# Attention of a hybrid transformer block: values become the stationary operand in two parts, the turned exponentials stream past them

## The reference, cut to what matters

```python
def window_sink_attention(q, k, v, kc, vc, sink):      # "A": 3 local key tiles + 2 context tiles
    ...
    s_loc = jnp.where(mask[None, :, None, None], s_loc, -jnp.inf)
    p = jax.nn.softmax(jnp.concatenate([s_loc, s_ctx, s_sink], -1), -1).astype(v.dtype)
    out = (jnp.einsum('bnkgqs,bnskd->bnqkgd', p[..., :w], vw)
           + jnp.einsum('bnkgqc,bckd->bnqkgd', p[..., w:w + lc], vc))

def global_block_attention(q, k, v, kc, vc):           # "B": all 8 + 2 key tiles
    def one_block(qblk):
        s = jnp.einsum('bqkgd,bskd->bkgqs', qblk, k_all).astype(F32)
        p = jax.nn.softmax(s, -1).astype(v_all.dtype)
        return jnp.einsum('bkgqs,bskd->bqkgd', p, v_all)

def ctx_attention(q, k, v, sink):                      # "C": context queries on 2 context tiles
    s = jnp.einsum('bqkgd,bskd->bkgqs', (q * ATTN_SCALE).reshape(bsz, lc, nkv, grp, hd), k)
    p = jax.nn.softmax(s, -1)[..., :lc].astype(v.dtype)
    return jnp.einsum('bkgqs,bskd->bqkgd', p, v)
```

## Time and profile before

| | |
|---|---|
| time, median of 3 runs | 3813.87 us (3808.86 to 3818.49) |
| the profiled execution's own time | 3815.01 us |
| its span | 3813.2 us |
| busy in the span: PE / DVE / ACT / POOL | 88% / 49% / 22% / 36% |
| mean granted clock | 0.944 |
| attention of layer 0: first score matmul, last exponentials | 262.2 us, 525.4 us |
| attention of layer 1: first score matmul, last output | 2284.9 us, 2528.3 us |

### The profile page before, as it was taken

How to read it: one execution, slowest core, us unless ns; L and a number is a source line. 1 busy time by engine, 2 the same in 40 slices (tenths; PEclk the granted TensorE clock), 3 DMA queues, 4 the chain that set the end, 5 groups by cost and what they waited for, 6 DMA issues and landing times. The chain is left out here.

```text
span 3813.2 us, 47769 instructions
## 1 busy us (share of the span) xinstructions
PE 3362.3 (88%) x17208; PEld 2793.3 (73%) x17208; DVE 1866.7 (49%) x2854; ACT 846.7 (22%) x1574; POOL 1386.0 (36%) x1032
## 2 busy tenths in 40 slices
PE   0969989877979999999997669989787799999997
PEld 0849878655858888888884549878666578888885
DVE  8976534678582222222227886525675532222225
ACT  1136432212041010000003226432211220010102
POOL 1354222253324333343432254213242344444443
PEclk9979999988989999999998789999888899999998
DMA  7500002002301111111011410011002011111111
GB/s 278 171 17 1 0 30 65 6 20 89 118 28 39 39 39 39 33 41 42 33 33 67 171 61 1 0 39 56 6 14 86 33 40 49 50 50 50 44 50 50
DMA packets 63857, 197.74 MB, mean 52 GB/s; under 512 B 6160, under 2 KB 16656, under 8 KB 62736
## 3 DMA queue, kind: packets, MB, share of 16 engines
q1 hardware_dynamic: 54736, 172.32, 13.3%
q10 hardware_dynamic: 9024, 24.14, 1.8%
HBM read 177.05 MB, written 19.40 MB: 52 GB/s over the span
## 5 line engine op out<-in xcount | busy, mean ns | idle before, releaser
L188 PE MATMUL ps<-h_hi,f_whi 128*128 128x512 f32 (+1 forms) x1760 | 650.8, 370 | 26.5 <-DVE h_lo L1917 19.7
L189 PE MATMUL ps<-h_lo,f_whi 128*128 128x512 f32 (+1 forms) x1760 | 650.0, 369 | 0.0
L190 PE MATMUL ps<-h_hi,f_wlo 128*128 128x512 f32 (+1 forms) x1760 | 649.4, 369 | 0.0
L2145 DVE TENSOR_TENSOR f_gated<-f_gated,ps 128x512 f32<-128x512 f32 (+1 forms) x110 | 69.6, 634 | 973.8 <-PE ps L190 968.5
L2029 POOL TENSOR_TENSOR f_whi<-f_wraw,small 128x1024 fp32r<-128x1024 f32 x128 | 251.8, 1967 | 608.1 <-PE ps L190 608.1
L2153 DVE SCALAR_TENSOR_TENSOR x_res<-ps,mod,x_res 128x512 f32<-128x512 f32 (+1 forms) x440 | 306.8, 697 | 242.2 <-PE ps L190 241.9
L188 PEld LDWEIGHTS ps<-h_hi,f_whi 128*128 128x128 f32 x1760 | 333.3, 189 | 85.8 <-issue 22.2
L190 PEld LDWEIGHTS ps<-h_hi,f_wlo 128*128 128x128 f32 x1760 | 333.0, 189 | 55.8
L189 PEld LDWEIGHTS ps<-h_lo,f_whi 128*128 128x128 f32 x1760 | 333.3, 189 | 55.2
L188 PE MATMUL ps<-f_ahi,f_whi 128*128 128x512 f32 (+1 forms) x880 | 328.3, 373 | 0.0
L189 PE MATMUL ps<-f_alo,f_whi 128*128 128x512 f32 (+1 forms) x880 | 323.5, 368 | 0.0
(11 more groups left out here) (219 smaller groups left out, 6212.8 us busy)
## 6 DMA issues: line engine op xcount, KB each, us to landing
f_wraw<-in_w_ffn SPq DMA_DIRECT2D x132, 512.0 KB, 3.2
ada_w<-in_w_ada SPq DMA_DIRECT2D x80, 512.0 KB, 3.5
wrawc<-in_w_in SPq DMA_DIRECT2D x26, 512.0 KB, 3.8
wrawab<-in_w_in SPq DMA_DIRECT2D x16, 512.0 KB, 4.4
wrawo<-in_w_out SPq DMA_DIRECT2D x16, 512.0 KB, 3.4
ada_w<-in_w_ada ACTq DMA_DIRECT2D x16, 512.0 KB, 4.4
x_res<-in_xT SPq DMA_DIRECT2D x8, 640.0 KB, 6.5
x_spill<-x_res ACTq DMA_DIRECT2D x8, 640.0 KB, 5.6
```

Source lines behind the costliest of these rows:

```text
L188: pe.matmul(out, w_hi, h_hi, start=first, stop=False)
L189: pe.matmul(out, w_hi, h_lo, start=False, stop=False)
L190: return pe.matmul(out, w_lo, h_hi, start=False, stop=last)
L2145: dve.tensor_tensor(g, g, pl.bank(3 + c, tn), ALU.mult).then_inc(u_taken[c], 1)
```

## The change

The value matmul is turned round. The values are stored in two float32r parts side by side, the rounded value and the rest, 64 + 64 columns: `v_tok` is now `[P, group, tile, kv head, 128]`. They are the stationary operand. The turned exponentials too are split in two parts, `turned[:, t, 0, :]` (rounded) and `turned[:, t, 1, :]` (the rest), 256 columns that stream past. One float32r matmul per key tile gives the four products, with the value parts on the partitions and the exponentials' parts in the columns. ACT copies this 128 x 256 block out of bank 7 to `quarters`, and two float32 matmuls with the constant `joiner` (two identities over each other) add the four quarters and bring the queries back to the partitions, in bank 6.

In the unit's terms: step 5 becomes an ACT copy of every group (`turned_high`) and a DVE subtraction of every group (`turned_rest`); step 6 becomes values, ACT `take_output`, PE `join`; the output of a unit comes one unit later on DVE. All turns of a unit lie in its own three banks and are issued together. `project_attention` splits the values the same way. Tiles move in SBUF to make room, the A tiles all are written out, and the residual is loaded back in three pieces, the last of them after the turning of `mix_ab`.

```diff
@@ attend, TensorE
             def values(w, g):
                 first, end = groups[w.kind][g]
-                if g == 0:
-                    pe.wait_ge(first_copied, w.u + 1)
-                    if not (w.static and w.u < 1):
-                        pe.wait_ge(o_done, w.u)
-                else:
-                    pe.wait_ge(later_copied, w.late + g)
+                wait_copied(w, g)
                 keys = w.keys()
-                col = 128 * w.group + HD * (w.h // 2)
                 for t in range(first, end):
-                    mm = pe.matmul(pl.bank(7, HD), turned[w.par][:, t * P:(t + 1) * P],
-                                   pl.v[:, keys[t], col:col + HD], start=(t == 0),
+                    mm = pe.matmul(pl.bank(7, 2 * P), pl.v[:, w.group, keys[t], w.h // 2, :],
+                                   turned[w.par][:, t, :, :].rearrange("p r q -> p (r q)"), start=(t == 0),
                                    stop=(t == len(keys) - 1))
+            def join(w):
+                if w.static and w.u == 0:
+                    pe.wait_ge(join_ready, 1)
+                pe.wait_ge(o_copied, w.u + 1)
+                if not (w.static and w.u < 1):
+                    pe.wait_ge(o_done, w.u)
+                for r in range(2):
+                    mm = pe.matmul(joined_at, quarters[:, r, :], joiner[:, :], start=(r == 0), stop=(r == 1))
+                mm.then_inc(joined, 1)
...
             def wait_copied(w, g):
+                pe.wait_ge(turned_in, w.all + (g + 1))
...  (score of w: the waits for its banks stand before each run of key tiles)
                 for place, tile, n in w.runs():
+                    if not (w.static and w.u < 2):
+                        v = w.step(-2)
+                        wait_copied(v, min((place + int(w.kind == "A")) // 4, len(groups[v.kind]) - 1))
...
             def body(w):
-                second, prev = w.step(2), w.step(-1)
+                second, prev, last_but_one = w.step(2), w.step(-1), w.step(-2)
+                before = len(groups[prev.kind]) if prev is not None else 0
                 for g in range(len(groups[w.kind])):
+                    transposes(w, g)
+                if last_but_one is not None:
+                    join(last_but_one)
+                for g in range(before):
+                    values(prev, g)
                 if second is not None:
                     score(second)
@@ attend, VectorE
+            def turned_rest(w, g):
+                dve.wait_ge(turned_hi, w.all + (g + 1))
+                dve.tensor_tensor(turned_part(w, g, 1), turned_source(w, g), raw(turned_part(w, g, 0)),
+                                  ALU.subtract).then_inc(turned_in, 1)
...
             def body(w):
-                nxt, prev = w.step(1), w.step(-1)
+                nxt, last_but_one = w.step(1), w.step(-2)
                 if nxt is not None:
                     maximum(nxt)
-                if w.kind != "A":
-                    copy_first(w)
-                if prev is not None:
-                    output(prev)
+                for g in range(len(groups[w.kind])):
+                    turned_rest(w, g)
+                if last_but_one is not None:
+                    output(last_but_one)
@@ attend, ScalarE
+            def turned_high(w, g):
+                act.wait_ge(t_full, w.all + (g + 1))
+                act.activation(turned_part(w, g, 0), turned_source(w, g), ACT.Copy).then_inc(turned_hi, 1)
+
+            def take_output(w):
+                act.wait_ge(pv_done, w.u + 1)
+                if not (w.static and w.u < 1):
+                    act.wait_ge(joined, w.u)
+                act.activation(quarters[:, :, :].rearrange("p r q -> p (r q)"), pl.bank(7, 2 * P), ACT.Copy) \
+                    .then_inc(o_copied, 1)
...
             def body(w):
+                if last_but_one is not None:
+                    take_output(last_but_one)
+                for g in range(min(2, len(groups[w.kind]))):
+                    turned_high(w, g)
                 if nxt is not None:
                     exponent(nxt)
+                for g in range(2, len(groups[w.kind])):
+                    turned_high(w, g)
@@ project_attention, ScalarE and VectorE
+                if at.kind == "v":
+                    act.wait_ge(ada.tile_done, at.i * 32 + ada.SLOTS)
+                    for g, c in enumerate(ORDER):
+                        act.wait_ge(turned, at.i * 3 + (g + 1))
+                        act.activation(v_part(at.i, c, 0), turned_v(g, c), ACT.Copy).then_inc(v_rounded, 1)
...
-                    dve.wait_ge(turned, i * 3 + (g + 1))
-                    dve.tensor_copy(...)
+                    dve.wait_ge(v_rounded, i * 3 + (g + 1))
+                    dve.tensor_tensor(v_part(i, c, 1), turned_v(g, c), raw(v_part(i, c, 0)), ALU.subtract) \
@@ gather_mix, SyncE
-        sp.dma_start(pl.x[:, :, 0:width], pl.x_dram[:, :, 0:width]).then_inc(x_in, 16)
+        for tiles_in in (slice(0, 2), slice(6, 8), slice(2, 6)):
+            if tiles_in.start == 2:
+                sp.wait_ge(turned, 4 * len(chunks))
+            sp.dma_start(pl.x[:, tiles_in, 0:width], pl.x_dram[:, tiles_in, 0:width]).then_inc(x_in, 16)
```

More of the change, by code:

```diff
@@ L165, in bank, with qk_slot @@
         return self.ps[:, 512 * b:512 * b + n]
+def qk_slot(t):
+    return {0: 2, 1: 3, 2: 0, 3: 4, 4: 5, 5: 1}[t]
 class Lead:
@@ L832, in attend, with turned_part, turned_source @@
     final = Unit(len(blocks) - 1, len(blocks) - 1, HEADS - 1)
+    joined_at = pl.bank(6, HD)
+    def turned_part(w, g, rest):
+        first, end = groups[w.kind][g]
+        return turned[w.par][:, first:end, rest, :]
+    def turned_source(w, g):
+        first, end = groups[w.kind][g]
+        return pl.bank(w.turned_bank(g), (end - first) * P).rearrange("p (t q) -> p t q", q=P)
     with nc.Block() as block:
@@ L912, in transposes @@
                     pe.wait_ge(p_done, w.u + 1)
-                before = None if w.own(g) else w.before_in_bank_6(g)
-                if before is not None:
-                    wait_copied(*before)
                 for t in range(first, end):
@@ L957, in _ @@
             over_units(pe, body)
+            join(final.step(-1))
             for g in range(len(groups[final.kind])):
                 values(final, g)
+            join(final)
         @block.vector
@@ L1024, in _ @@
             over_units(dve, body)
+            output(final.step(-1))
             output(final)
@@ L1054, in _ @@
             round_keys(1)
-            def body(w):
-                nxt = w.step(1)
-                for g in range(0 if w.kind == "A" else 1, len(groups[w.kind])):
-                    first, end = groups[w.kind][g]
-                    act.wait_ge(t_full, w.all + (g + 1))
-                    act.activation(turned[w.par][:, first * P:end * P],
-                                   pl.bank(w.turned_bank(g), (end - first) * P), ACT.Copy) \
-                        .then_inc(later_copied if g else first_copied, 1)
+            def turned_high(w, g):
[7 more added lines that the diff above has]
+                    .then_inc(o_copied, 1)
+            def body(w):
+                nxt, last_but_one = w.step(1), w.step(-2)
+                if last_but_one is not None:
+                    take_output(last_but_one)
+                for g in range(min(2, len(groups[w.kind]))):
+                    turned_high(w, g)
                 if nxt is not None:
                     exponent(nxt)
+                for g in range(2, len(groups[w.kind])):
+                    turned_high(w, g)
             over_units(act, body)
+            take_output(final.step(-1))
+            take_output(final)
 def project_ssd(pl, l, last):
```

123 lines of the change are left out of this document (47 added, 76 removed).

## The result

The changed kernel took 3833.59 us, the median of five runs (3832.26 to 3840.19), against 3813.87 us before. The ratio is 1.0051, with a 95% interval of 1.0038 to 1.0064: slower by 19.7 us. The profiled execution has a span of 3831.8 us beside 3813.2 before, so the two traces differ by 18.6 us and can be used for the accounting.

A forecast was written before the change was run, and what follows sets the result against it. TensorE was taken to bound A (five-tile) and B (ten-tile units) before the change. Terms 23.3 + 1 - 20.8 + 4 + 2 + 0.5 = +10, plus 1 for pipeline filling: +11 us, 3825 us; range 3808 to 3845.

The forecast's parts named there:

- A, 2.88 us, +23.3: Five-key-tile attention units: interval between exponentials grows from 2.45 to 2.88 us, 54 times 0.43, +23.3 us.
- the ring: In five-tile units: turns, ACT copy, DVE subtraction, then the next score waiting for that bank; 2.88 us a round.
- Rival 1: Five-tile units cost only DVE's list, 2.64 us each; 3812 us, not slower; chance 0.17.
- B, 4.47 and 4.52 us, -20.8: Ten-key-tile units: 4.47 us written out (-4.5 us in all), 4.52 in the loop (-16.3 us).
- The first units, +1, and +1 for the filling: Each layer's four half-clock units stay bounded by TensorE, +1 us together; filling a pipeline one step deeper, +1 us.
- C and the passages, +4: Two-key-tile units: DVE's list with hops makes 1.75 us in place of 1.50; 16 units, +4 us.
- The ends of the attention, 0: Stage end: last ten values 1.2 us shorter, copy, join and output behind them about as long; 0.
- The values' stage, +2: In `project_attention` ACT's rounding adds 0.38 us per wait and 0.60 at the end; +2 us over both layers.
- The residual's load, +0.5: Half the residual's load starts only when `mix_ab` is turned, mostly covered by DVE's splitting; +0.5 us, bounds 0 and +9.
- The clock, rival 4: TensorE's clock falls to half in five-tile or ten-tile units, adding 32 us; 3857 us; chance 0.06.
- Rival 2: TensorE stays the bound, all added work covered: five-tile units 2.35 us, ten-tile 4.0; 3766 us; chance 0.05.
- DVE over 90% busy in A: Sign expected in the profile after: DVE busy over 90% of the time in five-tile units.

The follow-up runs named there:

- the other execution of the old attention: The kernel before with only the residual loaded in three pieces, attention code unchanged: 3814.47 us; layer 0's first four A intervals took 13.27 us.
- the pair with GpSimd's wait: Kernel before and changed kernel, each with GpSimd's output-projection weight splits made to wait for VectorE's scaling of mix_c: 3799.39 and 3826.23 us.
- the three pieces alone: The kernel before with the residual loaded in three pieces, a wait between second and third, nothing else: 3814.47 us, ratio 1.0002.
- the three edits: Changed kernel with third turned copy ahead of the exponentials, five-tile units' turned tiles in their own place, GpSimd's splits behind the mix_c scaling: 3766.7 us.
- the kernel before with the same wait: The kernel before with GpSimd's output-projection weight splits started only when VectorE has scaled mix_c: 3799.39 us, ratio 0.9966.

## Why the prediction was right, and where not

The forecast was 3825 us, slower, and the time is 3834, inside the range. The place and the kind of both effects came out. The sum of its terms was +11 and the trace has +18.6, of which -7.4 is an escape I didn't foresee; against the +26 to +27 without it the sum was 15 us short. That the time came within 9 us of the forecast is therefore in part luck. Without the escape it would have been 3841 us, still inside the range, but near its upper end.

- **A, 2.88 us, +23.3.** Measured 2.96 and +27.6. The two parts of the ring that I read from rows were right: 298.93 less 297.86 is 1.07 us (forecast 1.09), 299.99 less 298.93 is 1.06 (1.07). From the subtraction to the next weight load are 0.81 us where I had 0.67 + 0.05. The hop into TensorE was the mis-sized link, by 0.09 us in every unit. Rival 1 fell for the reason given there: the score waits for the subtraction.
- **B, 4.47 and 4.52 us, -20.8.** Measured 4.50 and -20.0. Every link of the chain is in the trace above in the order of the forecast.
- **The first units, +1, and +1 for the filling.** Measured +7.1, or +9.5 against the other execution of the old attention. The step that failed is "bounded by TensorE either way". TensorE is idle there for 2.5 to 2.7 us at a time. I had priced the units and not what stands in DVE's list between them: `split_keys(1)`, 4.7 us, which before ran beside ACT's rounding and afterwards stood behind a subtraction that waits for ACT. The second interval alone, between the second and the third exponentials, went from 3.56 to 6.60 us in each layer, 6.1 us together. The clock's fall back behind that idle time comes on top: the third and fourth interval took 3.36 and 3.55 us in layer 0, 4.19 and 2.96 in layer 1, where the later ones take 2.94. The kernels' code shows this place, the diff shown above does not contain it; I did not walk through it instruction by instruction.
- **C and the passages, +4.** Measured +4.0.
- **The ends of the attention, 0.** Measured +3.2 (2.2 in the pair with GpSimd's wait), 2.6 of it in layer 0. From the last exponentials to the last output it went from 3.08 to 5.48 us in layer 0 and from 8.22 to 8.44 in layer 1: the added steps behind the last values were not covered by what the values save. No experiment is about it.
- **The values' stage, +2.** Measured +5.0. The wait ahead of the second turn is the row that answers to the earlier trace rows:

```profile
147.54 1.09 PE L465 MATMUL ps<-const,ab_vst 128*128 128x128 f32 x8 [1.57 <-DVE v_tok L575]
```

  It grew by 0.93 us where I had 0.38: not only the rounding came into the path but also a second hop between engines.
- **The residual's load, +0.5.** Covered: layer 0 is 14.9 us behind the kernel before in the scan (764.9 against 750.0 us) and 15.3 in the feed-forward part (1124.8 against 1109.5), and the three pieces alone gave 3814.47 against 3814.08 us.
- **The clock, rival 4.** Once the ring runs, the trace shows 1.00 in A with TensorE idle for 0.36 us in each 2.94. The rule that I quoted from the Trainium skill ("TensorE: Matmul & The Clock Gate", section "A second HAM failure mode: psum-queue depth-cycling") would have had it swing; it did not, and the trace decides. The clock did fall once per layer in the first units, behind 2.5 and 2.7 us in which TensorE stood idle. The prediction had no term for that.
- **Rival 2.** It said: if all added work were covered, A 2.35, B 4.0, 3766 us. With their waits taken out the stretches come to just that, A 2.41 and B 4.03. So the rival had priced what TensorE's list allows in A and B. That the three edits also end at 3766.7 us is chance: about 15 us of it come from GpSimd's wait, which the rival knew nothing of, and against the kernel before with the same wait the three edits are 33 us faster and not 48.
- **DVE over 90% busy in A** did not come: 50.04 of 60 us, 83%. In a ring no engine is full, which a check on busy shares alone would have missed.

## What to carry to other kernels

Add up the ring, not the lists: where an extra step is put between a buffer's fill and its release, it lengthens whatever waits for that buffer by its whole length and one hop, though every engine has room. Then look for the cheapest cut: an order of two instructions on one engine was worth 29 us in its stretch here, and another place in PSUM for a unit's turned tiles 31 in its own. And when work is moved behind a new wait, walk through the in-order list of that engine at the first and the last unit: a long job that used to fill a gap may now stand behind the wait.

## What the runs showed of the hardware

**VectorE and GpSimd in SBUF.** A scaling of 128x256, SBUF to SBUF, takes 340 ns alone and up to 2498 ns beside GpSimd's split. Parts of the kernel before, layer 1, scalings alone (us, DVE busy, PEclk, DMA share, GB/s):

```profile
2890.90:2892.30 1.40, 1.36 (x6) 0.50 0.99 383
...
2895.50:2896.80 1.30, 1.30 (x1) 1.00 1.02 391
...
2901.10:2902.90 1.80, 1.71 (x7) 0.50 1.02 421
```

Six start in 1.4 us before GpSimd, one in 1.3 us beside it, and the last seven in 1.7 us when it has ended. It can also fall the other way. In the changed kernel's layer 1 GpSimd's instruction was the one that stretched, from 1.9 to 3.17 us. The pairs seen in the profiles fall into two heaps: where GpSimd begins 1.4 to 1.6 us after the first scaling (eight cases), DVE loses 7.6 us; where it begins 2.8 to 3.3 us after it (four cases), DVE loses nothing. What the weights' landing depends on, and why the loser changes, stays open. The Trainium skill ("SBUF — State Buffer", section "Who interferes with whom") says that the two engines share a pair of ports that the earlier instruction holds until it ends, and that the order of issue decides who blocks. The trace agrees with the holding in the first heap, where single scalings last up to 2.5 us beside GpSimd's 1.9 to 2.3. In the second heap GpSimd's first instruction grows from 1.9 to 3.2 to 3.8 us and ends 1.75 us after the last scaling. DVE's train was first in both heaps, so the order of the two trains alone does not tell who loses.

The kernel before spread over 20 us in one series of executions (3801.04 to 3821.12), with the wait over 4.7 (3796.95 to 3801.61). A collision that comes and goes between executions would do that; I did not trace a second execution to show it. The place where the clock rises also differed between executions, as told above, and the one case seen was worth 2.4 us.

**One key tile of values.** Ten value matmuls of 256 float32r columns, each with a new stationary tile, fill 1.28 us in the B unit above (436.63 to the next score at 437.91). That is 0.13 us each, where two float32 records of 64 columns had taken 0.23: in the kernel before the ten records of the A unit at 282.78 start 0.11 us apart.
